# Empty steps ahead of three kinds of transposes, and the first unit's retention and attention at other steps

## The chip, the cores and the metric

The kernel runs on one core of a Trainium2 chip. The metric is the device time of one execution in microseconds (us); less is better. Before the change the median of three runs is 3471.58 us (3471.1 to 3473.25).

The engines are TensorE (PE in the rows; PEld is its weight load), VectorE (DVE), ScalarE (ACT), GpSimd (POOL) and SyncE (SP), each with its own stream of instructions in program order. They meet through semaphores. All data are float32.

## The reference

The program computes a two-layer encoder over 16 meta tokens and 1024 input tokens of width 1024. Cut to what matters here:

```python
h = layer_norm(concatenate([meta, x]), ln_in_g, ln_in_b)
for i in range(DEPTH):                       # DEPTH = 2
    proj = h @ w_in[i]
    p_conv, p_swa, p_ret, p_rwkv = split_cols(proj, IN_SIZES)
    y_conv = short_conv_mixer(p_conv, conv_w[i])
    y_swa = swa_mixer(p_swa, swa_sinks[i], cos_a, sin_a)     # windowed attention, softmax with a sink
    y_ret = retention_mixer(p_ret, cos_r, sin_r)             # chunkwise retention, then an RMS norm
    y_rwkv, v_first = rwkv7_mixer(p_rwkv, ...)               # recurrent, then a group norm
    h = layer_norm(ALPHA * h + concatenate([...]) @ w_out[i], ln1_g[i], ln1_b[i])
    h = layer_norm(ALPHA * h + conv_glu_ffn(h, ffn_w_up[i], ffn_conv_w[i], ffn_w_down[i]), ln2_g[i], ln2_b[i])
return h[:, N_META:]
```

## The kernel before

The tokens are cut into four chunks of 256 (the first has the 16 meta tokens as well, so 272), and a chunk of a layer is a unit: u = 0 to 7, the first four of layer 0. A unit has tiles of 128 tokens (chunk 0 has the tile of 16 as well). Activations lie with features on the partitions; `dense` multiplies one 512 KB weight tile (a slot) with a chunk in eight matmuls, which the profile counts as sixteen instructions. SyncE loads the weight tiles into five slots in their order of use.

Every engine runs the same plan as Python generators. `main` is a chain of dense features: for a unit u it is `mixer_out(u)`, then the input features of the next unit `project(u + 1)`, then `ffn(u)` with 44 up features and 22 pieces of the down projection. Each `yield` ends a **step**. Beside `ffn(u)` two **lanes** are advanced by one step after each step of the main program (`together`): `rwkv(u + 1)`, and a second lane, `side(u + 1)` (retention, then attention), then the normalisation and transposing of input tiles that are still missing (`input_tile`, tiles 5 to 8, beside the ffn of units 0 and 1), then the transposing of finished output tiles. So a lane's instruction stands on each engine behind the same dense feature of the main program. In a step of the up projection TensorE has a whole dense feature to do. The order in a step is main, rwkv lane, second lane.

There is nothing to run the first unit's lanes beside but its own projection: `alongside(chain(project(0), project_retention(1)), w_next, s_next)`. From the thirteenth feature on each dense feature is there cut into three steps (of three, three and two matmuls). The constants `RWKV_START`, `INPUT_START` and `SIDE_START` say at which step the rwkv lane, input tile 3 and retention begin. Attention begins 11 steps behind retention.

Three kinds of transposes on TensorE wait for a chain that ends on VectorE:

- In attention, per tile: TensorE makes the scores (`L1099`, semaphore `a_sc`); VectorE scales, masks and takes the maximum (`L1618` to `L1629`); ScalarE takes exponentials (`L669`); VectorE divides (`L1637`, semaphore `a_pn`); TensorE transposes the result, two steps behind the scores; ScalarE copies (`L676`); TensorE multiplies with the values (`L1115`).
- In an input tile: VectorE normalises rows (`L1229`, semaphore `in_norm`), TensorE transposes them one step behind the statistics, ScalarE copies.
- In the rwkv lane: the group norm of `YW` (`L1549` to `L1561`, semaphore `w_norm`), then the transposes.

All transposes are recorded under the helper's line `L764` and all dense features under `L770` (the down projection under `L1167`); the source tile tells them apart (`prpt` the attention weights, `hT` input rows, `YW` the rwkv result, `vbuf` the values). Attention first transposes the values in `vbuf` once a unit, which waits for `a_window`: this follows the last features of the unit's projection, their rotations (`L1451`, `L1452`, `L1400`) and the copies into `kbuf` and `vbuf` (`L1435` to `L1440`) on VectorE. The end of retention is a reciprocal and two products over 128x544 elements on VectorE (`L1604`, `L1606`, `L1608`). In the rwkv lane the state goes from one chunk of 64 to the next: TensorE multiplies (`L1005`), VectorE adds (`L1540`, semaphore `w_znew`), and the next product waits.

Of the kernel before, what the change touches and what calls it, by code (L numbers as in the profile page):

```python
# [34 lines left out]
def layer_of(u):  # L35
    return u // NCH
# [14 lines left out]
def nth_tile(u, j):  # L51
    return layer_of(u) * NT + j
# [56 lines left out]
        _last[SMALL_BANK[_name]] = _name  # L109


RWKV_START, INPUT_START, SIDE_START = 12, 21, 40


def all_blocks():
# [114 lines left out]
def chain(*programs):  # L230
    for program in programs:
        yield from program


def late(steps, program):
# [5 lines left out]
def build(nc, x, meta, weights, params, ln_in, consts, tables, out):  # L241
    with ExitStack() as ctx:
# [79 lines left out]
        def bank(b):  # L322
            return psum[:, b, :]
# [134 lines left out]
        def _(a):  # L458
# [8 lines left out]
            def input_tile(j):  # L467
                t0, n = TILES[j]
                a.wait_ge(S["in_mv"], j + 1)
                act(sd3[j % 3][:n], mv3[j % 3][:n, 1:2], ACT.Sqrt, bias=eps_ln[:n]).then_inc(S["in_sd"], 1)  # L470
                yield
                a.wait_ge(S["in_T"], j + 1)
                b = R0 + 2 * j if j < 3 else BX
                for k in range(4 if j < 3 else KD):
                    ins = act(hT[:, k, t0:t0 + n], bank(b + k // 4)[:, (k % 4) * P:(k % 4) * P + n], ACT.Identity,
                              bias=ln_in_sb[:, KD + k:KD + k + 1], scale=ln_in_sb[:, k:k + 1])
                ins.then_inc(S["in_hT"], 1)
                yield
# [110 lines left out]
            def rwkv(u):  # L589
# [41 lines left out]
                a.wait_ge(S["w_ssq"], u + 1)  # L631
                act(ws2[:, :4 * nt], ws1[:, :4 * nt], ACT.Sqrt, bias=eps_gn, scale=1.0 / HD).then_inc(S["w_sd"], 1)
                yield
                for i, (j, off, n) in enumerate(tiles_of(u)):
                    a.wait_ge(S["w_yT"], nth_tile(u, j) + 1)
                    act(mixT[:, 6:8, off:off + n], bank(R0 + i)[:, 0:256].rearrange("p (t s) -> p t s", t=2)[:, :, :n],
                        ACT.Copy).then_inc(S["w_yTc"], 1)
# [3 lines left out]
            def side(u):  # L641
# [14 lines left out]
                act(rsd[:, :, :n], psum[:, BX:BX + 2, :n], ACT.Sqrt, bias=eps_ret, scale=1.0 / HD).then_inc(S["r_sd"], 1)  # L656
                yield
                yield
                a.wait_ge(S["a_vt"], u + 1)
                vt = bank(BX).rearrange("p (b m k) -> p b m k", b=2, m=2)  # L660
                act(Vw[:, :, 0], vt[:, :, 0], ACT.Copy)
# [2 lines left out]
                for i, (j, off, n_) in enumerate(tiles):  # L664
                    nth, w = before + i, WIN if j else META
                    yield
                    a.wait_ge(S["a_max"], nth + 1)
                    for h in range(4):
                        ins = act(PR[:n_, h, :w], SC[:n_, h, :w], ACT.Exp, bias=nm[:n_, h:h + 1], accum_out=rsum[:n_, h:h + 1])  # L669
                    ins.then_inc(S["a_exp"], 1)  # L670
                    act(es[:n_], sk4[:n_], ACT.Exp).then_inc(S["a_es"], 1)
                    yield
                    a.wait_ge(S["a_pt"], nth + 1)
                    for m in range(2 if j else 1):
                        rows_m = min(w - P * m, P)
                        ins = act(PT[:rows_m, m, :, :n_], bank(BX + m).rearrange("p (h s) -> p h s", h=4)[:rows_m, :, :n_],  # L676
                                  ACT.Copy)
                    ins.then_inc(S["a_ptc"], 1)
                    yield
                    a.wait_ge(S["a_oT"], nth + 1)  # L680
                    act(mixT[:, 2:4, off:off + n_], bank(BX)[:, 0:2 * n_].rearrange("p (g s) -> p g s", g=2),
                        ACT.Copy).then_inc(S["a_mix"], 1)
                    yield
# [64 lines left out]
        def _(pe):  # L748
# [52 lines left out]
            def input_tile(j):  # L801
                t0, n = TILES[j]
                yield
                pe.wait_ge(S["in_norm"], j + 1)
                if j >= 3:
                    pe.wait_ge(S["in_hT"], j)
# [72 lines left out]
            def rwkv(u):  # L879
# [135 lines left out]
                    yield  # L1015
                yield
                yield
                pe.wait_ge(S["w_norm"], u + 1)
                for i, (j, off, n) in enumerate(tiles_of(u)):
                    for ct in range(2):  # L1020
# [6 lines left out]
            def side(u):  # L1027
# [52 lines left out]
                ins.then_inc(S["r_ssq"], 1)  # L1080
                yield
                yield
                pe.wait_ge(S["r_sd"], u + 1)
                pe.wait_ge(S["a_window"], u + 1)
                vt = bank(BX).rearrange("p (b m k) -> p b m k", b=2, m=2)
# [7 lines left out]
                for i, (j, off, n_) in enumerate(tiles):  # L1093
# [7 lines left out]
                    ins.then_inc(S["a_sc"], 1)  # L1101
                    yield
                    yield
                    pe.wait_ge(S["a_pn"], nth + 1)
                    for m in range(2 if j else 1):
                        rows_m = min(w - P * m, P)
# [93 lines left out]
        def _(v):  # L1200
# [14 lines left out]
            def input_tile(j):  # L1215
# [12 lines left out]
                v.wait_ge(S["in_mv"], j + 1)  # L1228
                ts(xin, xin, mv3[j % 3][:n, 0:1], rstd3[j % 3][:n], ALU.subtract, ALU.mult).then_inc(S["in_norm"], 1)  # L1229
                yield  # L1230
                if j < 3:
                    v.wait_ge(S["in_first"], 32)
                    v.wait_ge(S["in_T"], j + 1)
# [245 lines left out]
            def rwkv(u):  # L1479
# [80 lines left out]
                after(k)  # L1560
                tt(Y3, Y3, wide(ws3), ALU.mult).then_inc(S["w_norm"], 1)  # L1561
                yield
                yield
                v.wait_ge(S["w_yTc"], tiles_before(u) + nt)
                n = chunk_of(u)[1]
# [7 lines left out]
            def side(u):  # L1573
# [34 lines left out]
                tt(mixT[:, 4:6, :n], mixT[:, 4:6, :n], rsd[:, :, :n], ALU.mult).then_inc(S["r_mix"], 1)  # L1608
                yield
                yield  # L1610
                sink = par[:, layer_of(u) * NP_COLS + P_AT["sink"]:layer_of(u) * NP_COLS + P_AT["sink"] + 4]
                for i, (j, off, n_) in enumerate(tiles):
                    nth, w = before + i, WIN if j else META
# [5 lines left out]
                    else:  # L1619
# [17 lines left out]
                    tt(PR[:n_, :, :w], PR[:n_, :, :w], rden[:n_, :, None].broadcast_to([n_, 4, w]),  # L1637
                       ALU.mult).then_inc(S["a_pn"], 1)
                    yield
                    yield  # L1640
                    yield

# [208 lines left out]
```

## Time and profile before

| | |
|---|---|
| median of three runs | 3471.58 us |
| the profiled execution | 3472.48 us |
| its span, first to last instruction | 3470.4 us |
| TensorE busy | 3359.4 us, 97% of the span |
| VectorE busy | 1357.8 us, 39% |
| ScalarE busy | 878.8 us, 25% |
| mean granted TensorE clock | 0.988 of full speed |
| read from HBM | 426.22 MB, 124 GB/s over the span |

The profiled execution took 0.90 us longer than the median, and 2.1 us of it lie outside the span. An engine that is busy for 97% of the span leaves little to others; the rest is waits and the time that matmuls take longer at the lower clock.

### The profile page before, as it was taken

To read this page: it belongs to the slowest core of one execution; us is meant where nothing else is said; L and a number is where in the kernel's file an instruction comes from. 1 tells how busy PE (TensorE), PEld (TensorE's weight loads), DVE (VectorE), ACT (ScalarE), POOL (GpSimd) and SP (SyncE) were. 2 spreads that over 40 slices of the span, in tenths; PEclk is the share of its full clock that TensorE was granted. 3 is DMA by queue.
4 is the path that set the end of the run, shared out by engine and by line. 5 is a ranking of instruction groups with operands and counts; after the bars stand their busy time and mean duration, and the time that the engine had idled before them with its cause. 6 is when DMAs were issued, how large, how long until landed. Compare 5 with 4: busy or idle time off the path is not lost.

```text
span 3470.4 us, 51622 instructions
## 1 busy us (share of the span) xinstructions
PE 3359.4 (97%) x21652; PEld 2801.3 (81%) x21652; DVE 1357.8 (39%) x3285; ACT 878.8 (25%) x2648; POOL 37.9 (1%) x71
## 2 busy tenths in 40 slices
PE   8989999999999999999999999999999999998997
PEld 6768778887788878888888887788888888887886
DVE  4335433244323444153531535415344244433432
ACT  3223331123312232032420323204232043211211
POOL 0000000000000000000000000000000000000000
PEclk9999999999999999999999999999999999999998
DMA  6224233443344433443334433344334443344442
GB/s 195 64 88 134 92 98 129 150 136 96 104 140 152 134 98 117 151 137 125 104 116 140 135 121 103 117 146 136 120 116 128 158 134 109 117 134 134 146 152 97
DMA packets 128726, 433.76 MB, mean 125 GB/s; under 512 B 13280, under 2 KB 25696, under 8 KB 128368
## 3 DMA queue, kind: packets, MB, share of 16 engines
q1 hardware_dynamic: 127344, 426.28, 38.2%
q8 instruction: 172, 2.82, 0.3%
q0 software_dynamic: 1152, 4.19, 0.3%
q14 instruction: 58, 0.48, 0.0%
HBM read 426.22 MB, written 4.19 MB: 124 GB/s over the span
## 4 chain that ended last, share of the span: by engine, by line
PE 92%; DVE 4%; ACT 3%; issue 1%; DMA 0%; SPq 0%; DVEq 0%; POOL 0%; ACTq 0%; POOLq 0%
PE psum L770 61%; PE psum L1167 18%; PE psum L764 2%; PE psum L784 2%; PE psum L937 1%; PE psum L948 1%; PE psum L946 1%; ACT prpt L669 1%; PE psum L904 1%; ACT L669 1%; PE psum L962 1%; PE psum L1115 1%; DVE prpt L1637 0%; PE psum L1099 0%; PE psum L1070 0%
## 5 line engine op out<-in xcount | busy, mean ns | idle before, releaser
L770 PE MATMUL psum<-hT,slots 128*128 128x256 f32 (+1 forms) x8832 | 2041.5, 388 | 15.1 <-ACT hT L495 7.0
L770 PEld LDWEIGHTS psum<-hT,slots 128*128 128x128 f32 x8832 | 1660.8, 191 | 300.7 <-issue 37.2
L1167 PE MATMUL psum<-gT,slots 128*128 128x256 f32 (+1 forms) x2816 | 619.5, 382 | 0.0
L1167 PEld LDWEIGHTS psum<-gT,slots 128*128 128x128 f32 x2816 | 534.6, 190 | 82.2 <-issue 0.2
L707 ACT ACTIVATE last<-psum 128x2 f32<-128x2 f32 x352 | 60.0, 170 | 992.7 <-PE psum L770 992.7
L1244 DVE SCALAR_TENSOR_TENSOR hT<-hT,psum 128x256 f32<-128x256 f32 (+1 forms) x128 | 54.3, 425 | 641.8 <-PE psum L1167 535.0
L1682 DVE TENSOR_SCALAR tmpG<-raw,par 128x256 f32<-128x256 f32 (+1 forms) x176 | 62.5, 355 | 478.8 <-ACT raw L708 478.8
L770 PE MATMUL psum<-mixT,slots 128*128 128x256 f32 (+1 forms) x1024 | 229.1, 383 | 2.4 <-DVE hT L1244 1.8
L486 ACT ACTIVATE sqb<-hT 128x256 f32<-128x256 f32 (+1 forms) x128 | 50.6, 419 | 684.8 <-DVE hT L1262 659.3
L770 PEld LDWEIGHTS psum<-mixT,slots 128*128 128x128 f32 x1024 | 193.4, 190 | 36.8 <-issue 7.7
L1682 DVE TENSOR_SCALAR gT<-raw,par 128x256 f32<-128x256 f32 (+1 forms) x176 | 62.5, 355 | 350.7 <-ACT raw L708 350.6
L708 ACT ACTIVATE raw<-psum 128x256 f32<-128x256 f32 (+1 forms) x352 | 134.2, 381 | 0.0
L1686 DVE SCALAR_TENSOR_TENSOR tmpG<-raw,par,tmpG 128x256 f32<-128x256 f32 (+1 forms) x176 | 86.1, 489 | 6.3
L1686 DVE SCALAR_TENSOR_TENSOR gT<-raw,par,gT 128x256 f32<-128x256 f32 (+1 forms) x176 | 86.1, 489 | 6.3
L1684 DVE SCALAR_TENSOR_TENSOR gT<-raw,par,gT 128x256 f32<-128x256 f32 (+1 forms) x176 | 86.0, 489 | 6.3
L1684 DVE SCALAR_TENSOR_TENSOR tmpG<-raw,par,tmpG 128x256 f32<-128x256 f32 (+1 forms) x176 | 86.0, 489 | 6.3
L465 ACT ACTIVATE rows<-psum 128x256 f32<-128x256 f32 (+1 forms) x80 | 30.9, 387 | 202.8 <-PE psum L770 202.6
L495 ACT ACTIVATE hT<-hT,par 128x256 f32<-128x256 f32 (+1 forms) x128 | 65.0, 591 | 50.6 <-DVE hT L1281 50.6
L1302 DVE TENSOR_TENSOR gT<-rows 128x256 f32<-128x256 f32 (+1 forms) x56 | 24.1, 430 | 137.0 <-ACT rows L513 114.1
L948 PE MATMUL psum<-wset 64*64 64x64 f32 (+1 forms) x1328 | 77.1, 218 | 0.0
L700 ACT ACTIVATE tmpG<-tmpG 128x256 f32<-128x256 f32 (+1 forms) x176 | 74.1, 421 | 11.0 <-DVE tmpG L1686 10.6
L1676 DVE TENSOR_TENSOR gT<-gT,tmpG 128x256 f32<-128x256 f32 (+1 forms) x176 | 74.4, 422 | 1.2
(230 smaller groups left out, 2624.7 us busy)
## 6 DMA issues: line engine op xcount, KB each, us to landing
slots<-in_weights SPq DMA_DIRECT2D x792, 512.0 KB, 3.4
hT<-in_x SPq DMA_DIRECT2D x8, 512.0 KB, 5.0
out<-prpt POOLq DMA_DIRECT2D x8, 512.0 KB, 3.1
tab<-in_tables SPq DMA_DIRECT2D x6, 512.0 KB, 4.5
con<-in_consts SPq DMA_DIRECT2D x1, 1562.0 KB, 11.1
tab<-in_tables SPq DMA_DIRECT2D x2, 544.0 KB, 5.7
par<-in_params SPq DMA_DIRECT2D x2, 386.5 KB, 5.7
con<-in_consts SPq DMA_DIRECT2D x1, 66.5 KB, 1.9
```

Source lines behind the costliest of these rows:

```text
L669: ins = act(PR[:n_, h, :w], SC[:n_, h, :w], ACT.Exp, bias=nm[:n_, h:h + 1], accum_out=rsum[:n_, h:h + 1])
L700: act(tmpG[:, m % 2, :n], tmpG[:, m % 2, :n], ACT.Silu).then_inc(S["g_silu"], 1)
L708: act(buf[:, 2:2 + n], psum[:, i % 2, :n], ACT.Copy).then_inc(S["evA"], 1)
L764: return pe.transpose(dst, src, ident[:n, :n])
L770: ins = mm(psum[:, i % 2, :n], lhsT, rhs, start=k == 0, stop=k == len(pairs) - 1)
L784: ins = mm(psum[:parts, b, :n], lhsT, rhs, start=k == 0, stop=k == len(pairs) - 1)
L948: ins = mm(dst[cs, h, 1, :w], Y1[cs, h, :w], TT[cs, h, 1, :w], start=True, stop=True)
L1167: ins = mm(psum[:, i % 2, :n], w[:, e * P:(e + 1) * P], gT[:, k, :n], start=k == 0, stop=k == KF - 1)
L1676: tt(gT[:, m, :n], gT[:, m, :n], tmpG[:, m % 2, :n], ALU.mult).then_inc(S["glu"], 1)
L1682: k = step(ts(y, src[:, 2:2 + n], par[:, w + 2:w + 3], None, ALU.mult))
L1684: k = step(stt(y, src[:, 1:1 + n], par[:, w + 1:w + 2], y, ALU.mult, ALU.add))
L1686: stt(y, src[:, 0:n], par[:, w:w + 1], y, ALU.mult, ALU.add).then_inc(S["fconv"], 1)
```

## The change

Three things are done. (1) In all three engine programs an empty step (`yield`) is put ahead of the transposes of attention weights and of `YW` for every unit but the first (`if u`), and of input tiles for tiles 5 to 8 (`if j >= 5`): VectorE's empty step stands behind the end of its chain, TensorE's and ScalarE's ahead of the transposes and of their copy. (2) The first unit's retention begins at step 28 instead of 40, right behind input tile 4. (3) The first unit's attention begins at step 57 instead of 51, through a number of empty steps ahead of it.

```diff
-RWKV_START, INPUT_START, SIDE_START = 12, 21, 40
+RWKV_START, INPUT_START, SIDE_START, ATTENTION_START = 12, 21, 28, 57
...
+def until_attention(u):
+
+    for _ in range(ATTENTION_START - SIDE_START - 11 if u == 0 else 0):
+        yield
...
 # TensorE
             def input_tile(j):
                 t0, n = TILES[j]
                 yield
+                if j >= 5:
+                    yield
                 pe.wait_ge(S["in_norm"], j + 1)
...
                 yield
                 yield
+                if u:
+                    yield
                 pe.wait_ge(S["w_norm"], u + 1)
...
                 ins.then_inc(S["r_ssq"], 1)
                 yield
                 yield
+                yield from until_attention(u)
                 pe.wait_ge(S["r_sd"], u + 1)
                 pe.wait_ge(S["a_window"], u + 1)
...
                     ins.then_inc(S["a_sc"], 1)
                     yield
                     yield
+                    if u:
+                        yield
                     pe.wait_ge(S["a_pn"], nth + 1)
...
 # VectorE
                 ts(xin, xin, mv3[j % 3][:n, 0:1], rstd3[j % 3][:n], ALU.subtract, ALU.mult).then_inc(S["in_norm"], 1)
                 yield
+                if j >= 5:
+                    yield
...
                 tt(Y3, Y3, wide(ws3), ALU.mult).then_inc(S["w_norm"], 1)
                 yield
+                if u:
+                    yield
                 yield
                 v.wait_ge(S["w_yTc"], tiles_before(u) + nt)
...
                     tt(PR[:n_, :, :w], PR[:n_, :, :w], rden[:n_, :, None].broadcast_to([n_, 4, w]),
                        ALU.mult).then_inc(S["a_pn"], 1)
                     yield
+                    if u:
+                        yield
...
 # ScalarE
                     act(es[:n_], sk4[:n_], ACT.Exp).then_inc(S["a_es"], 1)
                     yield
+                    if u:
+                        yield
                     a.wait_ge(S["a_pt"], nth + 1)
```

No instruction is added or taken away; they only stand elsewhere. Lines shift: `L764` becomes `L777`, `L770` becomes `L783`.

Three places show how. The first is TensorE beside the ffn of unit 0, at the transposes of the attention weights of unit 1's first tile (`a_pn`). Before:

```order
L770 MATMUL psum<-hT,slots 128x272 [waits evA,slot4_loaded]
L770 MATMUL psum<-hT,slots 128x272 x7
L937 MATMUL psum<-wset 64x64 [waits w_ttc]
L937 MATMUL psum<-wset 64x64 x7
L764 MATMUL psum<-con,prpt 128x128 [waits a_pn]
L764 MATMUL psum<-con,prpt 128x128 x3
L764 MATMUL psum<-con,prpt 80x128 x4
```

And in the changed kernel:

```order
L783 MATMUL psum<-hT,slots 128x272 [waits evA,slot4_loaded]
L783 MATMUL psum<-hT,slots 128x272 x7
L952 MATMUL psum<-wset 64x64 [waits w_ttc]
L952 MATMUL psum<-wset 64x64 x7
L783 MATMUL psum<-hT,slots 128x272 [waits evA,slot0_loaded]
L783 MATMUL psum<-hT,slots 128x272 x7
L963 MATMUL psum<-wset 64x64 [waits w_y1m]
L963 MATMUL psum<-wset 64x64 x7
L777 MATMUL psum<-con,prpt 128x128 [waits a_pn]
```

One whole dense feature and one piece of the rwkv lane now stand between. The second place is VectorE in the first unit, where the rwkv state of tile 1 is passed on (`w_get` to `w_z`). Before:

```order
L1522 TENSOR_TENSOR wset<-psum,con 128x256 [waits w_get]
L1525 TENSOR_TENSOR wset<-psum,rows 128x2x2x64
L1530 TENSOR_TENSOR wset<-wset,small 128x128 [waits vec]
L1530 TENSOR_TENSOR wset<-wset,small 128x128
L1534 TENSOR_TENSOR wset<-wset,small 128x2x64 [waits w_gt1]
L1534 TENSOR_TENSOR wset<-wset,small 128x2x64
L1540 TENSOR_TENSOR Zb<-psum,wset 128x128 [waits w_z,w_fc]
L1540 TENSOR_TENSOR Zb<-psum,wset 128x128 [waits w_z]
```

And in the changed kernel:

```order
L1556 TENSOR_TENSOR wset<-wset,small 128x2x64 [waits w_gt1]
L1556 TENSOR_TENSOR wset<-wset,small 128x2x64
L1628 RECIPROCAL prpt<-prpt 128x544 [waits r_sd]
L1630 TENSOR_TENSOR prpt<-prpt,rows 128x544 [waits vec]
L1632 TENSOR_TENSOR mixT<-mixT,prpt 128x544 [waits vec]
L1562 TENSOR_TENSOR Zb<-psum,wset 128x128 [waits w_z,w_fc]
L1562 TENSOR_TENSOR Zb<-psum,wset 128x128 [waits w_z]
```

The end of retention has come in ahead of the state's two additions; before, it stood among the rotations ahead of `a_window`. The third place is TensorE in the first unit's attention, from the scores of tile 1 (`a_mix`) to the transposes of its weights (`a_pn`). Before:

```order
L1099 MATMUL psum<-kbuf,rows 128x208 [waits a_mix]
L1099 MATMUL psum<-kbuf,rows 128x208 x3
L770 MATMUL psum<-hT,slots 128x256 x2
L1005 MATMUL psum<-Zb,wset 64x64 [waits w_fc,w_znew,w_ets,w_gts]
L1005 MATMUL psum<-Zb,wset 64x64 x3
L1010 MATMUL psum<-Zb,wset 64x64 x4
L770 MATMUL psum<-hT,slots 128x256 [waits evA,slot2_loaded]
L770 MATMUL psum<-hT,slots 128x256 x2
L1005 MATMUL psum<-Zb,wset 64x64 [waits w_znew]
L1005 MATMUL psum<-Zb,wset 64x64 x3
L1010 MATMUL psum<-Zb,wset 64x64 x4
L764 MATMUL psum<-con,prpt 128x128 [waits a_pn]
```

And in the changed kernel, with the transposes of `YW` just ahead of the scores:

```order
L777 MATMUL psum<-con,YW 128x128 x4
L1117 MATMUL psum<-kbuf,rows 128x208 [waits a_mix]
L1117 MATMUL psum<-kbuf,rows 128x208 x3
L783 MATMUL psum<-hT,slots 128x256 x2
L783 MATMUL psum<-hT,slots 128x256 [waits evA,slot4_loaded]
L783 MATMUL psum<-hT,slots 128x256 x2
L777 MATMUL psum<-con,prpt 128x128 [waits a_pn]
```

The rwkv lane has ended by then, and five dense matmuls alone stand between.

## Rows read from the trace of the kernel before

**Rows 1.** The page: the span and the busy time of the engines.

```profile
span 3470.4 us, 51622 instructions
PE 3359.4 (97%) x21652; PEld 2801.3 (81%) x21652; DVE 1357.8 (39%) x3285; ACT 878.8 (25%) x2648; POOL 37.9 (1%) x71
```

**Rows 2.** TensorE's waits, whole span: released by, us, times, longest.

```profile
PE psum L764 <- DVE prpt L1637: 24.1, 15, 2.7
...
PE psum L764 <- DVE YW L1561: 9.9, 7, 2.5
```

**Rows 3.** The same view, 242 to 3190 us: units 1 to 7.

```profile
PE psum L764 <- DVE prpt L1637: 18.5, 12, 1.9
PE psum L764 <- DVE hT L1229: 10.9, 4, 3.0
PE psum L764 <- DVE YW L1561: 7.4, 6, 1.3
```

**Rows 4.** Waits of the DMA queue for weight tiles.

```profile
SPq L401 <- PE psum L770: 2591.5, 616, 21.0
```

**Rows 5.** Timeline of TensorE, 856 to 901 us: start, duration, idle before.

```profile
856.98 3.72 PE L770 MATMUL psum<-hT,slots 128*128 128x256 f32 x16
...
863.23 1.09 PE L764 MATMUL psum<-con,prpt 128*128 128x128 f32 x8 [1.93 <-DVE prpt L1637]
...
869.40 0.27 PE L1005 MATMUL psum<-Zb,wset 64*64 64x64 f32 x2
...
896.31 1.09 PE L764 MATMUL psum<-con,hT 128*128 128x128 f32 x8 [2.98 <-DVE hT L1229]
...
900.78 0.68 PE L937 MATMUL psum<-wset 64*64 64x64 f32 x16
```

**Rows 6.** Windows: stretch, length, TensorE busy, granted clock, DMA share, GB/s.

```profile
425.00:440.00 15.00, 13.29 (x85) 0.89 0.22 71
455.00:475.00 20.00, 17.00 (x104) 0.83 0.24 78
860.00:880.00 20.00, 17.15 (x108) 0.91 0.28 87
880.00:895.00 15.00, 11.72 (x88) 0.89 0.25 82
2960.00:2980.00 20.00, 18.07 (x132) 0.91 0.24 71
```

**Rows 7.** Timeline of VectorE beside the ffn of unit 2.

```profile
850.77 1.02 DVE L1618 SCALAR_TENSOR_TENSOR SC<-psum,con 128x832 f32<-128x832 f32 x1
...
857.09 0.42 DVE L1522 TENSOR_TENSOR wset<-psum,con 128x256 f32<-128x256 f32 x1 [1.00 <-PE psum L991]
```

**Rows 8.** Timeline of VectorE in the first unit.

```profile
139.49 0.29 DVE L1540 TENSOR_TENSOR Zb<-psum,wset 128x128 f32<-128x128 f32 x1 [0.66 <-PE psum L1005]
...
171.39 3.55 DVE L1604 RECIPROCAL prpt<-prpt 128x544 f32<-128x544 f32 x1 [0.18 <-ACT prpt L656]
...
176.38 0.44 DVE L1451 TENSOR_TENSOR rows<-rows,tab 128x272 f32<-128x272 f32 x1
...
179.59 0.19 DVE L1440 COPY vbuf<-vbuf 128x64 f32<-128x64 f32 x1
...
198.41 1.02 DVE L1618 SCALAR_TENSOR_TENSOR SC<-psum,con 128x832 f32<-128x832 f32 x1
```

**Rows 9.** Timeline of TensorE in the first unit.

```profile
141.08 0.27 PE L1005 MATMUL psum<-Zb,wset 64*64 64x64 f32 x2
...
179.93 1.09 PE L764 MATMUL psum<-con,vbuf 128*128 128x128 f32 x4 [5.60 <-DVE vbuf L1440]
...
185.52 1.56 PE L770 MATMUL psum<-hT,slots 128*128 128x256 f32 x6
...
189.53 0.26 PE L764 MATMUL psum<-con,prpt 16*16 16x16 f32 x4 [0.17 <-DVE prpt L1637]
...
204.71 1.12 PE L764 MATMUL psum<-con,prpt 128*128 128x128 f32 x8 [2.69 <-DVE prpt L1637]
```

More of the change, by code:

```diff
@@ L1082, in side @@
                 yield
+                yield from until_attention(u)
                 pe.wait_ge(S["r_sd"], u + 1)
@@ L1230, in input_tile @@
                 yield
+                if j >= 5:
+                    yield
                 if j < 3:
@@ L1562, in rwkv @@
                 yield
+                if u:
+                    yield
                 yield
@@ L1610, in side @@
                 yield
+                yield from until_attention(u)
                 sink = par[:, layer_of(u) * NP_COLS + P_AT["sink"]:layer_of(u) * NP_COLS + P_AT["sink"] + 4]
@@ L1639, in side @@
                     yield
+                    if u:
+                        yield
                     yield
```

## The prediction

> **What bounds the kernel now.** I read the page first: TensorE is busy for 3359.4 of 3470.4 us, VectorE for 1357.8 [rows 1]. So the time moves with what TensorE does not do, and with how fast its clock lets it work; an idle VectorE or ScalarE costs nothing by itself. Then the DMA queue's own waits, to see whether weights could be the next bound: 616 of the transfers waited for TensorE to give up a slot, 2591.5 us in all [rows 4]. The weights stand ready and wait for the engine; a TensorE that is 1% faster meets no bound there. Then TensorE's own waits. The longest total is that of the transposes of attention weights, 24.1 us in 15 waits, and YW's is 9.9 us in 7 [rows 2]. The same view over units 1 to 7 alone gives 18.5 us in 12 waits for attention, 10.9 in 4 for input tiles, 7.4 in 6 for YW [rows 3]: 36.8 us in 22 waits, none over 3.0 us. The first unit has the rest: 24.1 - 18.5 = 5.6 us for attention, 9.9 - 7.4 = 2.5 us for YW, and 5.60 us ahead of the values' transposes [rows 9].
>
> Last I looked at the clock behind the waits. The wait of 1.93 us at 863.23 is followed by a stretch at the lower of the two levels (1.2 instead of 2.4 GHz): from the transposes to the next piece of the rwkv lane it takes 869.40 - 863.23 = 6.17 us, where the same work (eight transpose instructions, one dense feature) takes 900.78 - 896.31 = 4.47 us at full clock, although 2.98 us of waiting stood ahead of that one [rows 5]. So the lower level cost 1.70 us there, and whether a wait of this size brings it is not fixed by its length. The granted clock of that window is 0.91, so 0.09 x 2 x 20 = 3.6 us of it were at half level, and a microsecond at half level cost 1.70 / 3.6 = 0.47 us. In units 1 to 7 five windows have it, all of them behind waits of the three kinds: 3.3 + 6.8 + 3.6 + 3.3 + 3.6 = 20.6 us at half level [rows 6].
>
> **The change in units 1 to 7.** The empty steps cost no instruction. On TensorE they put one dense feature of 3.7 us (16 instructions, first row of [rows 5]) between the point at which it now waits and the transposes. The producer is not moved against the main program within the same tile, since VectorE's empty step stands behind its chain. So each wait shrinks by what TensorE does in the extra step: at least 3.65 us against a longest wait of 3.0. All 22 should go: -36.8 us. The slimmest margin is the second input tile: 3.65 - 2.98 = 0.7 us, and there the order adds a piece of the rwkv lane on TensorE ahead of the transposes and a mask on VectorE, which about cancel. With the waits the half-level stretches behind them should go: 20.6 x 0.47 = 9.7 us. Together -46.5 us.
>
> The Trainium skill (TensorE: Matmul & The Clock Gate, Terms) prices such time at half of the throttled time: 20.6 / 2 = 10.3 us, 0.6 us more than by the rows. This case's row lies close to it, and I keep the row's 0.47.
>
> What is queued behind? ScalarE's copy (`L676`) moves with the transposes, so it does not stand waiting in front of an eviction. The later pieces of the second lane slide one step per tile against the rwkv lane. The softmax of the second tile now starts on VectorE behind the state block that begins at 857.09, and ahead of the state's addition. From 857.09: block 1.6 us (to the softmax's place), first half of softmax 2.7 (three sizes of `L1618` with small ones), the convolution of the next feature and its gate 1.7, addition 0.3: done near 863.4 [rows 7] (the start and the 1.02 us of `L1618`; the rest are estimates from like instructions). TensorE asks for it after one more dense feature: 856.98 + 3.65 + 0.8 + 3.65 = 865.1 [rows 5]. Cover of 1.7 us, so no new wait. The lanes get at most four steps longer and end well inside the 66 steps of an ffn. Cost: nothing.
>
> **The first unit, attention.** Attention no longer asks for `a_window` in the step in which VectorE still has the end of retention (5.0 us from 171.39 to 176.38) and then the rotations and copies (3.2 us to 179.59 and a copy) to do [rows 8]. The 5.60 us go. What was behind them in VectorE's queue, the mask for the rwkv lane's next product, stays behind the rotations and is late by about 1.0 us (estimate: rotations done 3.3 us later than their start, against one third of a dense feature, 1.6, and a product of 0.6). The transposes at 179.93 were also followed by the low clock: 179.93 to 185.52 is 5.6 us [rows 9] for work that at full clock I put at 3.65, so 1.9 us come back. Net -6.5 us.
>
> But the later attention loses its cover. From the scores to the transposes of tile 1 the chain over VectorE and ScalarE took 204.71 - 198.41 = 6.3 us [rows 8, 9]. Now only five dense matmuls stand there: three take 1.5 us (185.52, six instructions), so 2.5 us. That makes a wait of 3.7 us for tile 1, and some 3.5 for tile 2. Tile 0's chain took 189.53 - 185.52 = 4.0 us, of which 2.5 are covered: 1.5. The group norm of YW follows tile 0's softmax on VectorE and holds up ScalarE's copy for tile 0 too; I put it at 2.7 us, from the 2.5 of before. Sum 11.4 us, where 5.6 + 2.5 = 8.1 us stood: +3.3 us.
>
> **The first unit, retention.** Started 12 steps earlier its pieces stand beside rwkv tile 1 instead of tile 2, with the same TensorE work between them; those waits were nothing and stay so. Its end is the exception. Reciprocal and products, 5.0 us, come to stand on VectorE ahead of the state's first addition. This addition ran at 139.49 for 0.29 us, and TensorE asked for it at 141.08: 1.3 us of cover [rows 8, 9]. It is late by 4.35 us or more, so TensorE waits some 3.1 us. The bounds are nothing (if its sum were ready only later and the addition overtook it, which the order excludes) and 5.0. A wait that was there in tile 1's masks (1.2 us) loses some 0.6 us to retention's pieces. Net +2.5 us.
>
> **The clock of the first unit.** The attention waits of before had half level behind them too; I put its cost by the same 0.47 at 4 us. Now waits of 3.1, 3.7 and 3.5 us stand there with less work between: I take 6 to 6.5 us. Net +2.2 us.
>
> First unit together: -6.5 + 3.3 + 2.5 + 2.2 = +1.5 us, between -5 and +10.
>
> **Sum.** -46.5 + 1.5 = -45.0 us, against the profiled execution's 3472.5 us: 3427.5. The median of before is 0.9 us lower, so I say 3427 us, 1.3% faster. A difference of 0.2% (7 us) is about what can be told from no change.
>
> **The rivals.**
>
> A, the first unit costs what it can. Each of its waits of 3 to 4 us brings two low stretches instead of one, the group norm and tile 0 block each other in turn, the state waits 5.0 us: +10 us. Time 3436 us. For it speaks that TensorE has hardly anything but thirds of dense features between steps 57 and 70. 0.13.
>
> B, waits stay in part. TensorE arrives 3.65 us later, but since it no longer waits elsewhere, VectorE and ScalarE may be later too: they are given the slack of 36.8 us back only as long as they are not near their own limit. If a third of the waits and their clock stay, the gain is 31 - 1.5: 3443 us. Against it: VectorE is busy for 39% and sits idle ahead of most convolutions. 0.08.
>
> C, the change does not do what it says: the producers slide by a step with their transposes, so the distance stays. Then units 1 to 7 gain nothing, and the first unit decides: 3471 to 3475 us. Against it stands the order: one dense feature more between the a_pn wait and the scores on TensorE, none on VectorE ahead of `L1637`. 0.02.
>
> D, slower. The softmax that now stands ahead of the state's addition in units 1 to 7 makes TensorE wait there for the state. The cover is 1.7 us per unit; to eat 45 us in seven units the wait must be 6.4 us in each, so the chain on VectorE longer by 8.1 us than I add up. From there on the kernel is slower; with 10 us, at 3472 + 7 x 1.9 = 3485 us. An idle VectorE ahead of the block at 857.09 (1.00 us) speaks against it [rows 7]. 0.02.
>
> E, the low clock does not come back with the waits: it falls as often elsewhere. The waits alone give 36.8 - 1.5: 3437 us. Against it: all five windows lie behind these waits. 0.07.
>
> **The numbers.** My forecast, 3420 to 3434, has 0.68. The range 3418 to 3441 takes in A and E and leaves out B, C and D and some of the rest. Faster by over 0.2%: 0.96; within: 0.02; slower: 0.02.
>
> **What would show it.** In the waits of TensorE from unit 1 on, the groups by `a_pn`, `in_norm` and `w_norm` are empty or under 2 us in sum, and the granted clock reads 1.00 there throughout. In the first unit there is no wait for `vbuf`; a new one of some 3 us stands at a state product `L1020` released by `L1562`, right behind a RECIPROCAL; attention waits of 3 to 4 us stand twice near the end of its projection, and low clock behind them. I am wrong if new waits for evictions (ScalarE) or for the state appear in units 1 to 7, if half level shows where no wait was, or if the first unit ends more than 10 us later than I say.

## The result, and the profile after

The changed kernel takes 3426.6 us (median of 4 runs, 3424.59 to 3426.68), the kernel before 3472.41 us beside it (4 runs, 3471.1 to 3476.57). The ratio is 0.9865, 95% interval 0.9848 to 0.9882: 1.3% faster. The forecast was 3427 us.

The page, first lines; they answer to [rows 1]:

```profile
span 3424.9 us, 51622 instructions
PE 3349.8 (98%) x21652; PEld 2795.0 (82%) x21652; DVE 1358.1 (40%) x3285; ACT 881.0 (26%) x2648; POOL 38.0 (1%) x71
```

The span fell by 45.5 us, TensorE's busy time by only 9.6 us: about four fifths of the gain is time in which TensorE stood still before, one fifth is matmuls that take less time because the clock was granted. TensorE's waits from 238 to 3145 us, which are units 1 to 7, answer to [rows 3]:

```profile
PE psum L783 <- DVE hT L1266: 1.8, 10, 0.2
PE psum L783 <- ACT rows L521: 1.3, 7, 0.2
PE psum L783 <- ACT gT L471: 1.0, 1, 1.0
PE psum L783 <- ACT vbuf L580: 0.2, 1, 0.2
```

This is the whole answer. The three groups of [rows 3] are gone, all 22 waits, and nothing has come in their place. The granted clock of that stretch (the fourth column from the right):

```profile
238.00:3145.00 2907.00, 2898.93 (x18747) 2424.25 (x18746) 1169.02 (x2826) 754.17 (x2260) 29.41 (x49) 1.00 0.40 128
```

In the first unit the timeline of TensorE shows these waits:

```profile
96.49 1.97 PE L777 MATMUL psum<-con,hT 128*128 128x128 f32 x8 [1.62 <-DVE hT L1249]
...
153.79 0.37 PE L1020 MATMUL psum<-Zb,wset 64*64 64x64 f32 x2 [2.92 <-DVE Zb L1562]
...
196.84 0.66 PE L777 MATMUL psum<-con,vbuf 128*128 128x128 f32 x4
...
203.32 0.25 PE L777 MATMUL psum<-con,prpt 16*16 16x16 f32 x4 [1.36 <-DVE prpt L1662]
...
209.23 0.88 PE L777 MATMUL psum<-con,YW 16*128 16x16 f32 x6 [1.08 <-DVE YW L1583]
...
217.41 1.09 PE L777 MATMUL psum<-con,prpt 128*128 128x128 f32 x8 [4.04 <-DVE prpt L1662]
...
230.77 1.09 PE L777 MATMUL psum<-con,prpt 128*128 128x128 f32 x8 [3.57 <-DVE prpt L1662]
...
244.00 1.31 PE L783 MATMUL psum<-mixT,slots 128*128 128x272 f32 x5
```

The values' transposes (196.84) no longer wait, where 5.60 us stood [rows 9]. One wait is new, for the state (153.79). Those of attention grew: tile 1 waits 4.04 us (217.41) where it waited 2.69 [rows 9], tile 2 waits 3.57 (230.77) and tile 0 1.36, and YW's fell from 2.5 to 1.08 us. VectorE's timeline shows what the first waits for:

```profile
148.47 3.55 DVE L1628 RECIPROCAL prpt<-prpt 128x544 f32<-128x544 f32 x1
152.05 0.72 DVE L1630 TENSOR_TENSOR prpt<-prpt,rows 128x544 f32<-128x544 f32 x1
152.81 0.72 DVE L1632 TENSOR_TENSOR mixT<-mixT,prpt 128x544 f32<-128x544 f32 x1
153.45 0.28 DVE L1562 TENSOR_TENSOR Zb<-psum,wset 128x128 f32<-128x128 f32 x1
```

The end of retention stands ahead of the state's addition, as the order had it.

**Where the time went, unit by unit.** The start of `mixer_out` (the first matmul from `mixT` of a unit in TensorE's timeline) cuts the span. The first three columns of numbers are of the profiled execution of each kernel, the last is the median of its executions. Here and below, "half level" is (1 - granted clock) x 2 x length, summed over windows of 10 us from 240 us to the end of unit 7's stretch.

| kernel | first unit, to | units 1 to 7 | half level in them | median, us |
|---|---|---|---|---|
| before | 241.73 | 2925.50 | 20.4 | 3472.41 |
| after | 244.00 | 2877.42 | 0 | 3426.6 |
| steps only | 244.74 | 2877.40 | 0 | 3424.99 |
| moves only | 242.19 | 2931.71 | 34.0 | 3479.61 |
| retention at 31 | 237.88 | 2877.39 | 0 | 3421.16 |
| 31 and 53 | 236.09 | 2877.39 | 0 | 3418.40 |
| attention's steps only | 241.62 | 2896.93 | 3.4 | 3444.22 |
| input tiles' only | 240.36 | 2907.90 | 6.8 | 3453.32 |
| YW's only | 239.87 | 2916.86 | 20.4 | 3464.56 |
| softmax slides | 244.06 | 2877.46 | 0 | 3423.53 |
| double step | 241.72 | 2876.13 | 0 | 3422.9 |
| 31, 53, one more | 236.75 | 2877.39 | 0 | 3420.23 |
| 31, 53, two more | 227.60 | 2877.41 | 0 | 3410.08 |
| 31, 51, two more | 236.29 | 2877.40 | 0 | 3417.98 |

The column "units 1 to 7" is the stretch from the start of `mixer_out(0)` to that of `mixer_out(7)`, beside which the lanes of units 1 to 7 run; I keep calling it units 1 to 7. From before to after it lost 48.08 us, the first unit took 2.27 more. The rest of the span, 303 us, is the same within 0.3 us. (The heading of [rows 7] says the ffn of unit 2: counted by these starts the rows lie beside that of unit 1, where the lanes work on unit 2. No number hangs on it.) Without the waits units 1 to 7 take 2877.4 us in eight of the nine programs that have all the empty steps, and 1.3 us less in the ninth.

### The profile page after: what moved, and what is told of

The parts are those of the page before. It is cut to its first block, busy times and chain, and to the rows that moved or that the text cites. A ratio compares the mean times of both kernels' runs of the same rounds, so it can differ in the third digit from the quotient of the medians.

```text
span 3424.9 us, 51622 instructions
## 1 busy us (share of the span) xinstructions
PE 3349.8 (98%) x21652; PEld 2795.0 (82%) x21652; DVE 1358.1 (40%) x3285; ACT 881.0 (26%) x2648; POOL 38.0 (1%) x71
## 4 chain that ended last, share of the span: by engine, by line
PE 96%; DVE 2%; ACT 1%; issue 0%; DMA 0%; SPq 0%; POOL 0%; DVEq 0%; POOLq 0%; ACTq 0%
PE psum L783 65%; PE psum L1187 18%; PE psum L777 2%; PE psum L797 2%; PE psum L952 1%; PE psum L963 1%; PE psum L961 1%; PE psum L919 1%; PE psum L977 1%; PE psum L1135 1%; PE psum L1117 0%; PE psum L1087 0%; PE psum L988 0%; ACT hT L503 0%; PE psum L1090 0%
## 5 line engine op out<-in xcount | busy, mean ns | idle before, releaser
L783 PE MATMUL psum<-hT,slots 128*128 128x256 f32 (+1 forms) x8832 | 2038.0, 387 | 15.2 <-ACT hT L503 7.0
L783 PEld LDWEIGHTS psum<-hT,slots 128*128 128x128 f32 x8832 | 1655.9, 191 | 300.0 <-issue 37.7
L783 PE MATMUL psum<-mixT,slots 128*128 128x256 f32 (+1 forms) x1024 | 229.1, 383 | 2.4 <-DVE hT L1266 1.8
L783 PEld LDWEIGHTS psum<-mixT,slots 128*128 128x128 f32 x1024 | 193.4, 190 | 36.8 <-issue 7.7
## 6 DMA issues: line engine op xcount, KB each, us to landing
con<-in_consts SPq DMA_DIRECT2D x1, 1562.0 KB, 10.9
```

The costliest lines, as they stand in the source:

```text
L783: ins = mm(psum[:, i % 2, :n], lhsT, rhs, start=k == 0, stop=k == len(pairs) - 1)
```

## The experiments

All are variations of the changed kernel. They ran in three groups of four, each beside the kernel before on the same chip, whose median was 3471.7 us for experiments 1 to 4, 3473.34 us for 5 to 8 and 3470.01 us for 9 to 12. The ratios are to that median; times of different groups can be compared to about 3 us.

**1. Steps only.** `SIDE_START` and `ATTENTION_START` back at 40 and 51.

```diff
-RWKV_START, INPUT_START, SIDE_START, ATTENTION_START = 12, 21, 28, 57
+RWKV_START, INPUT_START, SIDE_START, ATTENTION_START = 12, 21, 40, 51
```

> The empty steps in units 1 to 7 alone; retention at step 40 and attention at step 51 as before. My theory (all of the gain is the waits of units 1 to 7 and their clock, the moves in the first unit about cancel): 3425 us, units 1 to 7 as in the changed kernel, the first unit as before with its 5.6 us wait for the values' transposes, so 1 to 2 us faster than the changed kernel. Rival (the moves of the first unit carry part of the gain): 3432 us or more.

3424.99 us (3423.43 to 3427.25), ratio 0.9867 (0.9854 to 0.9881). The whole gain is the empty steps'. The two moves of the first unit give nothing beside them: the 1.6 us between this kernel and the changed one lie inside the spread of both (3423.43 to 3427.25 and 3424.59 to 3426.68).

**2. Moves only.** All the `if u:` and `if j >= 5:` steps taken out, 28 and 57 kept.

> Retention at step 28 and attention at step 57 alone, no empty steps. My theory: 3474 us (+1.5), no wait for vbuf, a new one of 3 us for the state's addition, attention waits of 4 and 3.5 us. Rival (the moves pay by themselves): 3465 us.

3479.61 us (3477.06 to 3480.28, 10 runs), ratio 1.0023 (1.0014 to 1.0032): slower by 7.9 us, where 1.5 were expected. Between the two profiled executions the table has 0.46 us in the first unit and 6.21 us in units 1 to 7, whose order is that of before, with the same waits (18.5, 10.9 and 7.4 us in 12, 4 and 6). What differs is the clock behind them. The same attention transposes of unit 3 in TensorE's timeline of before:

```profile
1284.80 1.09 PE L764 MATMUL psum<-con,prpt 128*128 128x128 f32 x8 [1.93 <-DVE prpt L1637]
1285.73 3.62 PE L770 MATMUL psum<-hT,slots 128*128 128x256 f32 x16
```

and of this kernel, with the window around them:

```profile
1288.15 1.89 PE L771 MATMUL psum<-con,prpt 128*128 128x128 f32 x8 [1.93 <-DVE prpt L1646]
1289.83 4.54 PE L777 MATMUL psum<-hT,slots 128*128 128x256 f32 x16
...
1280.00:1300.00 20.00, 18.07 (x172) 15.04 (x169) 7.19 (x20) 8.09 (x25) 0.00 (x0) 0.91 0.27 81
```

The wait is 1.93 us in both. Behind it the eight transposes take 1.09 us in one and 1.89 in the other, and the dense feature 3.62 and 4.54. Half level is 13.6 us more over units 1 to 7 and the time 6.21 us more: 0.46 us for each. By stretches from one `mixer_out` to the next, the two that got a single low stretch more (3.4 us) took 1.67 and 1.66 us longer, 0.49 us for each; another with 6.8 us more took 2.81 us longer, 0.41 for each. Whether the low clock follows a wait of about 2 us is thus not fixed by the order of the instructions. The two programs start units 1 to 7 half a microsecond apart; that such a shift decides it is my reading, not shown.

Nor is it fixed by the program. Of the nine executions of the kernel before in the third group, seven took 3468.93 to 3472.04 us at a mean granted clock of 0.988 to 0.990, and two took 3479.66 and 3480.86 us at 0.986. All ten of the kernel with the moves only took 3477.06 to 3480.28 us.

**3 and 4. Other starts.** Retention at 31, with attention at 57 and at 53.

```diff
-RWKV_START, INPUT_START, SIDE_START, ATTENTION_START = 12, 21, 28, 57
+RWKV_START, INPUT_START, SIDE_START, ATTENTION_START = 12, 21, 31, 57
...
+RWKV_START, INPUT_START, SIDE_START, ATTENTION_START = 12, 21, 31, 53
```

> The changed kernel with retention at step 31 instead of 28, so that its reciprocal stands on VectorE behind both of the state's additions. My theory (the new wait at the state product is the reciprocal ahead of the addition): that wait of 2.9 us is gone with its low clock, 3422.5 us, 4 us faster than the changed kernel. Rival (the reciprocal is 5.0 us of VectorE wherever it stands, and holds up the next masks instead): the wait reappears at the first product of the next tile, 3426.5 us.

> Retention at step 31 and attention at step 53. My theory (attention at 57 has lost the rwkv lane as its cover, the rotations need only about two steps): no wait for vbuf or under 1 us, attention's and YW's waits 8 instead of 11.3 us, low clock less; 3419 us. Rival (the end of the projection is what attention waits for, with any start before 57): a wait of 2 us or more for vbuf, 3422.5 us or more.

3421.16 us (3420.34 to 3423.44), ratio 0.9858 (0.9843 to 0.9873), and 3418.40 us (3417.55 to 3419.67), ratio 0.9848 (0.9835 to 0.9861). At 31 the reciprocal stands behind the state's additions, in the timeline of VectorE:

```profile
148.02 0.29 DVE L1562 TENSOR_TENSOR Zb<-psum,wset 128x128 f32<-128x128 f32 x1 [3.29 <-PE psum L1020]
150.11 3.55 DVE L1628 RECIPROCAL prpt<-prpt 128x544 f32<-128x544 f32 x1 [1.59 <-ACT prpt L666]
```

TensorE's wait of 2.92 us is gone, and half level is gone there too (no low clock from 110 to 200 us). Of the rival 0.6 us came true: the waits for the masks (`L961`) went from 1.9 to 2.5 us. With attention at 53 the transposes of YW and of tile 0 wait no more, and two waits of attention, 4.00 and 4.05 us, are left. That is 6.6 us less than experiment 1 of the same group, so the start steps do matter, only not the ones that the change chose.

**5 to 7. Each kind of step alone**, with 40 and 51, so that the first unit is as before.

> Only the empty steps of attention, with retention and attention of the first unit at their old steps (40 and 51). My theory (each kind of wait goes by itself, and the low clock that stood behind it goes with it): the 12 waits of 18.5 us go, input tiles keep 10.9 us in 4, YW keeps 7.4 us in 6; with about 5 us of low clock and 1 us that the weight loads lose beyond the matmuls at each wait, 3471.7 - 24.5 = 3447 us. Rival one (the clock is bought back only when all waits go): 3453 us. Rival two (units 1 to 7 gain something that no single kind of step gives): this and the next two together gain much less than the 46.7 us of all the steps together.

> Only the empty steps of input tiles 5 to 8, the first unit as before. My theory: 4 waits of 10.9 us go and 3 to 6 us of low clock behind them in units 1 and 2 (the largest of the half-level windows, 6.8 us, lies there): 3456 us. Without the clock: 3461 us.

> Only the empty steps of the rwkv group norm, the first unit as before. My theory: 6 waits of 7.4 us go, none of them has low clock of its own behind it: 3464 us. If the low clock behind the attention waits hangs on the nearby waits of YW too, it may go by 2 to 5 us more: 3460 us.

3444.22 us (ratio 0.9917, 0.9903 to 0.993), 3453.32 us (0.9949, 0.9937 to 0.9962) and 3464.56 us (0.9975, 0.9964 to 0.9985). TensorE's waits over units 1 to 7, first of the kernel with attention's steps:

```profile
PE psum L773 <- DVE hT L1241: 8.8, 4, 3.0
PE psum L773 <- DVE YW L1573: 7.5, 6, 1.3
```

then with those of the input tiles:

```profile
PE psum L773 <- DVE prpt L1652: 18.6, 12, 1.9
PE psum L773 <- DVE YW L1575: 7.5, 6, 1.3
```

Each kind of step takes away its own waits. Attention's steps also push the input tiles to another place, which saves 2.1 us of theirs (10.9 to 8.8). The gains in units 1 to 7 are 28.57, 17.60 and 8.64 us, together 54.8, where all steps at once give 48.1. The sum is too large by what is counted twice: those 2.1 us, and the clock. Attention's steps bring half level from 20.4 to 3.4 us, input tiles' from 20.4 to 6.8, together 30.6 us where only 20.4 exist; the surplus 10.2 x 0.46 is 4.7 us. 2.1 + 4.7 = 6.8, against 6.7. So three low stretches of units 1 and 2 went with either cure. Two readings remain: each hung on more than one wait, or the low clock was only drawn otherwise in the profiled executions. The second can't be ruled out: two of the five executions of experiment 6 took 3457.79 and 3461.31 us at a mean granted clock of 0.989, the profiled one 3453.13 at 0.992. YW's steps alone left half level at 20.4, but not in the same places (a stretch at 2540 us is new, that at 2960 is gone): their 8.64 us are 7.4 us of waits and 0.2 us for each of six.

Rows show where these 0.2 us lie. Before, with a wait of YW, and in experiment 7, without it (the ends of matmuls in such rows are modelled):

```profile
2220.24 14.93 PE L770 MATMUL psum<-hT,slots 128*128 128x272 f32 x64
2236.21 0.66 PE L764 MATMUL psum<-con,YW 128*128 128x128 f32 x4 [1.04 <-DVE YW L1561]
...
2214.07 18.60 PE L779 MATMUL psum<-hT,slots 128*128 128x272 f32 x80
2232.51 0.60 PE L773 MATMUL psum<-con,YW 128*128 128x128 f32 x4
```

Without the wait the transposes begin 0.16 us ahead of the end of the dense matmuls (2232.67) and take 0.60 us instead of 0.66. With it this overlap is lost on top of the 1.04 us.

**8. The producer slides too.** VectorE's empty step of attention is put ahead of the division instead of behind it.

```diff
                     tt(sk4[:n_], sink[:n_], nm[:n_], ALU.add).then_inc(S["a_max"], 1)
                     yield
+                    if u:
+                        yield
                     v.wait_ge(S["a_exp"], nth + 1)
...
                        ALU.mult).then_inc(S["a_pn"], 1)
                     yield
-                    if u:
-                        yield
```

> All empty steps with retention and attention at their old steps, but in attention VectorE's empty step stands ahead of the end of its chain (between the maximum and the division), not behind it: TensorE and ScalarE still take the transposes and the copy a step later. No work is left out. My theory (what a step buys is the distance between producer and consumer in the main program's order): the end of the softmax slides with its transposes, which find it as late as before; the 12 waits stay with 1.5 us each and some low clock behind them, 3425 + 18.5 + 4 = 3447 us. Rival (what counts is the distance of the transposes from the scores, since VectorE has slack of its own): 3425 us, as with all steps behind the chain.

3423.53 us (3422.61 to 3426.62), ratio 0.9858 (0.9845 to 0.9872). My theory fell, the rival's number held: no wait for `a_pn` is left in units 1 to 7. Attention of unit 2 in the timelines of VectorE and TensorE, first with the steps behind the chain (experiment 1):

```profile
852.38 1.02 DVE L1662 TENSOR_TENSOR prpt<-prpt,small 128x832 f32<-128x832 f32 x1
...
856.41 1.04 PE L777 MATMUL psum<-con,prpt 128*128 128x128 f32 x8
```

and with the division a step later:

```profile
852.16 0.35 DVE L1709 TENSOR_SCALAR gT<-raw,par 128x256 f32<-128x256 f32 x1 [2.33 <-ACT raw L721]
...
853.47 0.28 DVE L1562 TENSOR_TENSOR Zb<-psum,wset 128x128 f32<-128x128 f32 x1
853.67 0.15 DVE L1660 TENSOR_TENSOR small<-small 128x4 f32<-128x4 f32 x1
...
854.07 1.02 DVE L1664 TENSOR_TENSOR prpt<-prpt,small 128x832 f32<-128x832 f32 x1
...
855.74 1.04 PE L777 MATMUL psum<-con,prpt 128*128 128x128 f32 x8
```

The slid division ends at 855.09, 0.65 us ahead of TensorE, the other at 853.40, 3.0 us ahead. In the first case VectorE was ready and idle for the division until the exponentials came. In the second it first does the convolution of the next feature. Its eviction was released when TensorE had finished that feature (ScalarE's `raw` at 852.1), while the transposes stand behind one more feature. So VectorE's step runs one dense feature ahead of TensorE's same step. What was late before was the chain from the scores over ScalarE (in experiment 1 VectorE stood idle for 1.47 us until ScalarE's part was done, ahead of the reciprocal and the division), not the place of the division.

**9. Double step.** A second empty step ahead of attention's transposes in units 1 to 7, first unit as before.

> As with the steps alone (old steps 40 and 51 in the first unit), but two empty steps ahead of the attention transposes in units 1 to 7, so two dense features more than before stand between. My theory (a step takes away only a wait that is there; beyond that it neither costs nor gives): units 1 to 7 take 2877.4 us again, the time is 3425 us. Rival (the later softmax meets the rwkv state on VectorE, or the lanes become too long for an ffn): waits at the state's products, 3430 us or more.

3422.9 us (3422.07 to 3423.63), ratio 0.9857 (0.9841 to 0.9874); units 1 to 7 take 2876.13 us. Once the wait is gone, more distance brings nearly nothing (1.3 us of 2877) and costs nothing.

**10 to 12. Steps in the first unit's attention as well.** Retention at 31, attention at 53. `if u:` is dropped, so that the first unit has one step too (10), and a second step is put in for unit 0 (11); 12 is 11 with attention at 51. The edit of 11, in all three engine programs:

```diff
-                    if u:
-                        yield
+                    yield
+                    if u == 0:
+                        yield
```

> Retention at step 31, attention at 53, and the empty step ahead of the attention transposes in the first unit as well; a step is there only a third of a dense feature (1.5 us). With starts 31 and 53 alone, two attention waits of 4.0 us stood in the first unit, and low clock behind them. My theory (the wait shrinks by what TensorE does in the step): two waits of 2.5 us, the low clock mostly as before: 3418.4 - 3.0 = 3415.5 us. Rival (the first unit's waits only move to the copies on ScalarE or to YW): 3418.5 us.

> As the one before with two empty steps in the first unit (one in the others). Two waits of 1 us are left, with less low clock: 6 us of waits and 2 to 4 us of the clock are gained against starts 31 and 53 alone: 3410 us. Rival: attention then ends too late and the output projection waits for its last result: 3415 us or more.

> As the one before, with attention at the old step 51. The transposes of the values come 3 us earlier; with the end of retention out of the way on VectorE (start 31) they find the values about ready: a wait of up to 1.5 us there, and 3 us more room at the end. 3410 to 3411 us. Rival: the wait for the values comes back with 3 us and more and low clock behind it: 3414 us.

3420.23 us (3419.55 to 3422.9), 3410.08 us (3409.81 to 3411.27) and 3417.98 us (3416.57 to 3418.91); ratios 0.9851 (0.9835 to 0.9868), 0.9821 (0.9805 to 0.9837) and 0.9843 (0.9827 to 0.9859). Number 11 came out at the expected time and is the best of all, though not by the expected parts: against experiment 4 TensorE's waits in the first unit fell by 2.8 us, where 6 were expected, and half level from 17.0 to 6.8 us, of which 3.4 lie ahead of attention and are not the steps'. Number 10 went to its rival. TensorE's timeline, without the further steps (experiment 4):

```profile
202.57 1.97 PE L777 MATMUL psum<-con,prpt 128*128 128x128 f32 x8 [4.00 <-DVE prpt L1662]
...
218.07 1.97 PE L777 MATMUL psum<-con,prpt 128*128 128x128 f32 x8 [4.05 <-DVE prpt L1662]
```

with one (10), and behind it ScalarE and VectorE of the same kernel:

```profile
207.30 1.44 PE L776 MATMUL psum<-con,YW 16*128 16x16 f32 x6 [7.95 <-DVE YW L1581]
...
203.27 1.28 ACT L640 ACT_TABLE_LOAD   x1
...
205.69 0.30 ACT L640 ACTIVATE small<-small,con 128x12 f32<-128x12 f32 x1 [1.13 <-DVE small L1576]
...
203.77 1.02 DVE L1660 TENSOR_TENSOR prpt<-prpt,small 128x832 f32<-128x832 f32 x1
204.71 0.94 DVE L1576 TENSOR_REDUCE small<-wset 128x12 f32<-128x768 f32 x1
...
206.29 0.96 DVE L1581 TENSOR_TENSOR YW<-YW,small 128x768 f32<-128x768 f32 x1
```

with two (11):

```profile
201.93 1.34 PE L778 MATMUL psum<-con,YW 16*128 16x16 f32 x6 [2.44 <-DVE YW L1585]
...
218.12 1.09 PE L778 MATMUL psum<-con,prpt 128*128 128x128 f32 x8 [1.42 <-DVE prpt L1664]
```

In number 10 attention's softmax of tile 1 and the group norm of YW come to the same step. The group norm's second sum on VectorE (204.71) stands behind the softmax's division (203.77), which waits for four exponentials on ScalarE; only then come the root on ScalarE (205.69, its table loaded at 203.27) and VectorE's last product for YW (206.29). So the transposes of YW wait for both chains in a row, 7.95 us. With two steps the second sum goes ahead of the division (199.34 and 204.46), and the two chains overlap. In number 12 they collide again (7.22 us for YW, 4.8 more than in 11), and the values wait 2.52 us at step 51, where up to 1.5 were expected. Together that is 7.3 us more than in 11, whose median is 7.9 us lower.

## Why the prediction was right

**Units 1 to 7, the waits: -36.8 us.** As said, all 22 are gone. Experiments 5 to 7 give each kind its own part.

**Units 1 to 7, the clock: -9.7 us.** It came back; the granted clock is 1.00 throughout. Its price, 0.47 us per microsecond from one pair of rows, measured 0.46 over units 1 to 7 of experiment 2. (The pair gives 0.50 when the low stretch is read from windows of 10 us, 3.4 us, instead of 3.6 from the rounded 0.91 of 20 us.) The Trainium skill (TensorE: Matmul & The Clock Gate, Terms) takes half of the throttled time; the stretches of experiment 2, 0.41 to 0.49, lie a little under that.

Waits and clock are 36.8 + 20.4 x 0.46 = 46.2 of the 48.08 us measured. The forecast of -46.5 was short by 1.6 us. What it lacks is mostly the cost of a YW wait beyond its length, a term that the prediction put at nothing. Three stretches between `mixer_out` starts, from 1070.95, 1907.39 and 2335.70 us before, have full clock before and after, so they show it free of the clock: they got 13.35 us shorter for 12.9 us of waits. In the same three, attention's steps alone gave 8.95 us for 9.2 us of waits, so an attention wait is worth no more than its length; YW's steps alone gave 2.75 us for 2.37 in the first two of them. Six YW waits at 0.2 make 1.2 us. The rest, 0.7 us, is about what the price of the clock leaves open (0.49 instead of 0.46 would be 0.6 us).

**The cover of 1.7 us** of the state behind the second softmax. In unit 2 of the changed kernel the addition runs at 849.49 for 0.28 us, and TensorE comes to its product at 851.51: 1.7 us. Both ends of it were 0.7 us later than summed, which cancels: from the start of the state block (842.81) the addition was done after 7.0 us, not 6.3 (VectorE stood idle for 0.89 us ahead of the convolution), and TensorE came after 8.7, not 8.0. The steps cost nothing there, as said, and experiment 9 found no cost in a further one.

**The first unit, attention.** The waits for which I summed 11.4 us are 1.36 (tile 0), 1.08 for YW and 1.29 for the copy of tile 0, 4.04 and 3.57: 11.3 us. `vbuf`'s 5.6 us are gone, and the late mask is 1.27 us for my 1.0.

**The first unit, retention.** The state waits 2.92 us, for 3.1. Experiment 3 took that wait away by the start step alone.

**The first unit, clock and sum.** I said +1.5 us, the two profiles differ by 2.27. Of these 1.25 us are there before the change can act: the input tile's transposes that wait 1.62 us stand at 95.24 and at 96.49 us, and TensorE's order is the same up to there; 1.0 us came behind them. One pair of profiles can't tell this: in the seven programs whose first unit has the order of before (before, steps only, experiments 5 to 9) it ends at 239.87 to 244.74 us, 242.0 in the mean; the two with 28 and 57 end at 242.19 and 244.00. The difference of the means, +1.1 us, agrees with +1.5 and also with nothing. The waits behind those transposes add up to 15.3 us before and 16.8 after, +1.5, where my terms for waits sum to +1.2 (-5.6 + 1.0 + 3.3 + 3.1 - 0.6). The term that was mis-sized is the clock's. After the change half level is 3.3 us behind the state's wait and 6.9 us behind attention's (windows from 150 to 165 and from 215 to 238 us, granted clock 0.89 and 0.85), which at 0.46 is 4.7 us, where I had 6 to 6.5. And before it was 17.2 us from 170 to 240 us, 7.9 us of time, where I had 1.9 + 4 = 5.9. So the clock of these waits gave back 3.2 us, where I had it cost 0.3. Against that the low clock between 90 and 110 us, which is not the change's, was 3.4 us longer (+1.6), and about 1 us is in no row. The total of 3427 us hit so closely partly by luck: units 1 to 7 gained 1.6 us more than I said, and the first unit lost 0.8 us more.

**The rivals.** A: the first unit's waits were 3 to 4 us as forecast, with less low clock than I had allowed for, and the state waited 2.92 us, not 5. B: no wait stayed. C, that a sliding producer would keep the waits, did not apply, and experiment 8 shows that it would not have cost what I said: my sentence "each wait shrinks by what TensorE does in the extra step" holds even with the division a step later, as long as VectorE is one feature ahead. The reason I gave against C was sound for this order, but the rule that I took into experiment 8, that distance in the common plan is distance in time, is wrong. D and E: in units 1 to 7 there is no wait for the state and no half level at all.

Among the expectations the largest miss beside experiments 8, 10 and 12 was that the moves alone would cost 1.5 us. I had left out that the 22 waits can be followed by another number of low stretches. And the 1 us that the expectation of experiment 5 lays to weight loads is shown by no run: its own stretches at full clock gave no more than the length of attention's waits.

## What to carry to other kernels

When several engines run one plan in lockstep and the busiest waits a little for short chains, look at what stands between request and result on the busiest engine: an empty step that lets one more independent piece of work in was free here, and took away the clock's loss behind the wait as well. Count distance in time on each engine from the trace, since an engine with slack can run ahead of the others in the same step of the plan (by a dense feature in experiment 8); and where two chains need the same two helper engines, keep them in different steps, or one queues behind the other (7.95 us of waiting in experiment 10, 2.44 in 11). Gains of several cures need not add up (54.8 us one by one, 48.1 together): measure them together.

## What the hardware showed that I had not expected

- The same wait of 1.93 us at the same place of the same order was followed by full clock in one program and by half level in another (experiment 2). Between those programs the number of low stretches differs enough to cost 6.2 us, with no other difference in units 1 to 7; executions of one program differ as much (3468.93 and 3480.86 us for the kernel before).
- A stretch of 2877.4 us with no wait over 1 us repeats within 0.1 us from program to program (eight of nine); the first 240 us, with waits of 1 to 11 us for loads and chains, vary by 5 us between programs of the same order.
- The low clock of the first unit was not the waits' length times a factor: behind 2.92 us of waiting at 153.79 the clock was low (0.89 from 150 to 165 us), behind 2.98 us in [rows 5] it was full. Nor was a wait always worth its length: YW's cost 0.2 us more, attention's did not.
